# Down projection of a gated MLP from seven block products per pair of tiles, its token sums made during the up projection and its weight sums on the vector engine

## The chip, the cores and the metric

One core of a Trainium2 chip. The time is the device time of one execution in microseconds; the kernel before was run three times, and the median counts. One further execution was profiled. Everything is fp32.

## The reference, cut to what matters

The program is a block of a conformer/RWKV model followed by a two-layer block with attention and experts. The change touches the end of the first block only, its convolution-gated MLP over T = 16 + 512 = 528 tokens, with a width of 1024 and D_FF = 2816:

```python
def conv_gated_mlp(h, ffn_up, ffn_dw, ffn_down):
    u = causal_dwconv(h @ ffn_up, ffn_dw)
    return (jax.nn.silu(u[..., D_FF:]) * u[..., :D_FF]) @ ffn_down

h = layer_norm(ALPHA * h + conv_gated_mlp(h, ffn_up[l], ffn_dw[l], ffn_down[l]), ln2_g[l], ln2_b[l])
```

## The kernel before, in words

Activations lie with channels on the 128 partitions and tokens along the free dimension: `h` is 8 tiles of 128 x 528, the gated activation (`F_`) is 22 tiles (FT = 22). Tokens are cut into two halves of C1 = 264. Each engine has its own instruction queue, written out in order; semaphores tie them together. SP (SyncE) issues the weight transfers, PE (TensorE) multiplies, ACT (ScalarE) copies out of PSUM and computes silu, DVE (VectorE) does the rest and POOL (GpSimd) some weight sums.

**Weights** come in slabs into two slots of SBUF, in turn (`stream`, L330). A slab is requested when the slab before the last, which had the same slot, has been multiplied.

**The up projection** (`Seven`) treats 22 pairs of output tiles. A pair (the two halves of the gated unit for tile m) has a 2 x 2 block of weights (two halves of the contraction by two output tiles) and two token halves, so it is a 2 x 2 by 2 x 2 block product. It is made from seven products of half the contraction (4 weight tiles) each, in this order on PE (`seven_products`, products on L466): M1 into bank a, M2 into bank b, M6 added to a, M5 into c, M7 added to a, M3 added to c, and a last one added to a. Some products take sums of weight blocks, of token blocks or both. The weight sums are s1, s2, s3 (`seven_first_sums`, L427, L429, L430) and s4 (`seven_last_sum`, L437, in place, after M2); POOL makes them in the up projection. The token sums t1 to t4 (`token_sum`) DVE makes once ahead of the up projection. ACT copies the bank away after M1, M6 and M5 (`seven_copy`, L498), since the next product is added to it; DVE combines: c11 (L511) after M2, c22 (L518) after M7, c12 (L524) after M3; ACT takes c21 at the end (L2811). The last product of a pair waits for c22 to have read bank a.

Per pair DVE then runs six taps of the causal convolution for the pair before (`ffn_taps`, L3103 and L3106), ACT its silu (L2800), and DVE the gating multiplication one pair later (`ffn_gate`, L3091, counted by `ffn_f`). Halves (`up_u`) and tap results (`up_conv`) have four buffers each.

**Between the projections** PE makes 16 transposes of the context (L2608, into banks 4 to 7), and ACT copies six of its eight tiles away (L2816).

**The down projection** is `Dense`: 8 output tiles, one weight tile column of 22 x 128 x 128 (1408 KB) as a slab for each; per output tile PE runs 2 token halves x 22 products (L371) after it has waited for all 22 gated tiles. ACT copies each output tile (L2820) and DVE adds it to `ALPHA * h` (L3124, counted by `res2`). The layer norm behind it begins on PE (L553) when all eight are added.

Of the kernel before, what the change touches and what calls it, by code (L numbers as in the profile page):

```python
# [184 lines left out]
def build(nc, I, out):  # L185
# [69 lines left out]
    def pc(name, i=0, p1=P):  # L255
# [30 lines left out]
        "ffn_up": Seven(11, 4, KT, two, dmas=2), "ffn_down": Dense(8, 1, FT, two),  # L286
# [167 lines left out]
    def seven_products(pe, p, sums, x, t, cn, t0, first=None, between=None):  # L454
# [4 lines left out]
        block = seven_landed(pe, p)  # L459
        s1, s2 = sums(p)  # L460

        def product(bank, w, v, fresh, k0=None):
            for k in range(h):
                if k0 is not None and first:
                    pe.wait_ge(*first(k0 + k))
                mm = pe.matmul(PS[:, bank, 0:cn], w[:, k, :], v[:, k, :], start=fresh and k == 0, stop=k == h - 1,  # L466
                               skip_group_check=not fresh)
            return mm
# [8 lines left out]
        pe.wait_ge(S("sv_t"), t0 + 2)  # L477
# [5 lines left out]
        pe.wait_ge(S("sv_t"), t0 + 3)  # L483
# [5 lines left out]
        pe.wait_ge(S("sv_t"), t0 + 4)  # L489
# [43 lines left out]
    def halves(ap):  # L533
        return ap.rearrange("p (c n) -> p c n", c=2)
# [1637 lines left out]
    UP_T, UP_S = CS, BNS  # L2172
    UP_C = UP_S + 4 * KT // 2 * P
    assert UP_C + 3 * C1 <= TMP
# [16 lines left out]
    def _(sp):  # L2191
# [81 lines left out]
        def ffn_src(n, dst):  # L2273
# [8 lines left out]
        stream(sp, "ffn_down", lambda n, dst: [(  # L2282
            dst[:, 0:FT * P].rearrange("p (k n) -> p k n", k=FT),
            down[:, :, n * P:n * P + P] if isinstance(n, int) else down[:, :, ds(n * P, P)])])
# [11 lines left out]
    def _(pe):  # L2296
# [314 lines left out]
        products(pe, "ffn_down", lambda k, c0, cn: at(F_ + k * T1 + c0, cn), [(S("ffn_f"), FT)])  # L2611
# [3 lines left out]
    def _(act):  # L2615
# [187 lines left out]
        for m, p in enumerate(ffn7):  # L2803
# [5 lines left out]
            if m >= 4:  # L2809
                act.wait_ge(S("ffn_conv"), 2 * (m - 4) + 2)  # L2810
# [7 lines left out]
        for k in range(KT - 2):  # L2818
            ctx_take(k)
        take(act, "ffn_down", lambda i, acc, j: nc.scalar.activation(halves(at(i * T1 + UB, T1)), acc, ACT.Copy),  # L2820
             pre=[(S("ffn_f"), FT)])
# [39 lines left out]
    def _(dve):  # L2861
# [217 lines left out]
        V.memset(A[:, UB:UB + 8 * UW].rearrange("p (i t) -> p i t", t=UW)[:, :, 0:FFN_K - 1], 0.0).then_inc(S("ffn_zero"), 1)  # L3079
# [13 lines left out]
        def ffn_taps(m):  # L3093
            dve.wait_ge(S("sv_c"), 2 * ffn7[m].g + 2)
            dve.wait_ge(S("acc_free"), FREE0 + ffn7[m].tile + 2)
            if m >= 4:
                dve.wait_ge(S("ffn_f"), m - 3)
# [10 lines left out]

        for m in range(FT):
# [4 lines left out]
            if m >= 4:  # L3114
                dve.wait_ge(S("ffn_conv"), 2 * (m - 4) + 2)
# [6 lines left out]
        for i in range(KT):  # L3122
            dve.wait_ge(*taken("ffn_down", i + 1))
            V.scalar_tensor_tensor(out=at(hk(i), T1), in0=at(hk(i), T1), scalar=ALPHA, in1=at(UB + i * T1, T1),  # L3124
                                   op0=ALU.mult, op1=ALU.add).then_inc(S("res2"), 1)
# [37 lines left out]
```

## Time and profile before

| What | Value |
|---|---|
| median of 3 runs | 4442.01 us (4436.71 to 4442.95) |
| profiled execution, own time | 4433.85 us |
| its span | 4431.7 us |
| PE busy | 4145.6 us, 94% of the span |
| DVE busy | 1463.7 us, 33% |
| ACT busy | 1031.9 us, 23% |
| POOL busy | 558.0 us, 13% |
| up projection, about | 1084 to 1361 us |
| down projection, about | 1367 to 1526 us |

The span is from the first to the last profiled instruction; the execution's own time is 2.2 us longer. Engine shares are averages over all stages, so for a change in one stage its own stretch has to be read. In the profile one fp32 product of 128x128 by 128x264 appears as two MATMUL records. LDWEIGHTS (PEld) overlaps the products. "Idle before" names the time that an engine stood before an instruction and what released it.

### The profile page before, as it was taken

The numbers are of one execution on the slowest core, as the hardware profiler recorded it, in microseconds if no ns is written. First come the engines' busy times: TensorE is split into PE (matmuls) and PEld (weight loads), VectorE is DVE, ScalarE is ACT, GpSimd is POOL, SyncE is SP. The second block draws the span as 40 slices with busy tenths as digits, with TensorE's granted clock in tenths as the row PEclk, the third lists the DMA queues.
The fourth block names the chain that finished last, engine by engine and source line by source line (L and its number), as shares of the span: only waits on it lengthen the run. The fifth ranks groups of instructions, "written<-read, shape, count | busy, mean of one in ns | idle before, by whom it ended". The sixth has DMA issues, their size and how long they took to land. (4 is left out here: it accounts for less than half of the span.)

```text
span 4431.7 us, 64143 instructions
## 1 busy us (share of the span) xinstructions
PE 4145.6 (94%) x28308; PEld 2685.2 (61%) x28308; DVE 1463.7 (33%) x2272; ACT 1031.9 (23%) x2070; POOL 558.0 (13%) x476
## 2 busy tenths in 40 slices
PE   7999999999999989898999979999899989969888
PEld 5888789887888745555555533333355468843332
DVE  1385854352441112415633410000314064421112
ACT  2112522211110131514311221221314052121111
POOL 0000023101441000001223210100000024400000
PEclk9999999999999999999999989999999999989999
DMA  2584300212222212010011299999311101279997
GB/s 88 179 282 158 87 23 4 81 57 71 93 79 66 77 35 64 20 43 20 20 57 59 98 356 386 384 386 391 101 57 46 43 27 70 95 302 427 426 427 313
DMA packets 191429, 664.55 MB, mean 150 GB/s; under 512 B 11558, under 2 KB 75750, under 8 KB 166582
## 3 DMA queue, kind: packets, MB, share of 16 engines
q1 hardware_dynamic: 184950, 638.24, 38.0%
q0 software_dynamic: 6208, 22.27, 1.7%
q8 instruction: 222, 3.64, 0.3%
q14 instruction: 49, 0.40, 0.0%
HBM read 638.85 MB, written 20.05 MB: 149 GB/s over the span
## 5 line engine op out<-in xcount | busy, mean ns | idle before, releaser
L371 PE MATMUL psum<-arena 128*128 128x264 f32 (+4 forms) x3936 | 1026.6, 422 | 38.9 <-ACT arena L1301 19.1
L466 PE MATMUL psum<-arena 128*128 128x264 f32 (+2 forms) x3696 | 945.8, 418 | 12.5 <-ACT arena L2792 6.7
L371 PEld LDWEIGHTS psum<-arena 128*128 128x128 f32 x3936 | 747.2, 191 | 304.9 <-issue 123.1
L466 PEld LDWEIGHTS psum<-arena 128*128 128x128 f32 x3696 | 700.1, 190 | 255.1 <-issue 13.5
L1191 PE MATMUL psum<-arena 128*64 128x512 f32 x3072 | 700.2, 602 | 44.3 <-DMA arena<-in_w_e 37.5
L1191 PEld LDWEIGHTS psum<-arena 128*64 128x64 f32 x3072 | 212.3, 138 | 469.5 <-issue 429.4
L2060 DVE TENSOR_TENSOR arena<-arena,psum 128x512 f32<-128x512 f32 x32 | 22.0, 688 | 802.6 <-PE psum L1197 543.9
L869 PE MATMUL psum<-arena 128*128 128x512 f32 x544 | 235.7, 592 | 0.0
L2415 PE MATMUL psum<-arena 64*64 64x64 f32 x7424 | 225.9, 219 | 8.1 <-issue 4.5
L2415 PEld LDWEIGHTS psum<-arena 64*64 64x64 f32 x7424 | 224.0, 135 | 11.2 <-issue 8.4
L498 ACT ACTIVATE arena<-psum 128x384 f32<-128x384 f32 (+2 forms) x234 | 99.2, 424 | 494.8 <-PE psum L466 466.8
L1197 PE MATMUL psum<-arena 128*32 128x256 f32 x3072 | 185.7, 382 | 0.0
L869 PEld LDWEIGHTS psum<-arena 128*128 128x128 f32 x544 | 103.2, 190 | 128.5 <-issue 127.7
L437 POOL TENSOR_TENSOR arena<-arena 128x512 f32<-128x512 f32 (+1 forms) x78 | 105.6, 1354 | 571.2 <-PE psum L466 571.2
L1197 PEld LDWEIGHTS psum<-arena 128*32 128x32 f32 x3072 | 90.0, 109 | 127.4 <-issue 77.9
L2885 DVE SCALAR_TENSOR_TENSOR arena<-arena 128x528 f32<-128x528 f32 x240 | 164.8, 761 | 0.0
L2078 DVE SCALAR_TENSOR_TENSOR arena<-psum,arena 128x512 f32<-128x512 f32 (+1 forms) x96 | 66.9, 706 | 187.5 <-PE psum L1158 169.0
L427 POOL TENSOR_TENSOR arena<-arena 128x512 f32<-128x512 f32 (+1 forms) x78 | 95.2, 1221 | 251.8 <-DMA arena<-in_ffn_up 239.3
L518 DVE TENSOR_TENSOR arena<-arena,psum 128x384 f32<-128x384 f32 (+2 forms) x78 | 36.7, 471 | 245.4 <-PE psum L466 245.4
L2370 PE MATMUL psum<-arena 128*128 128x264 f32 x512 | 117.4, 387 | 0.0
L1575 ACT ACTIVATE arena<-psum,arena 64x512 f32<-64x512 f32 x64 | 43.7, 683 | 291.7 <-PE psum L1197 165.6
L2370 PEld LDWEIGHTS psum<-arena 128*128 128x128 f32 x512 | 96.1, 189 | 19.2 <-ACT arena L2701 2.5
(378 smaller groups left out, 3847.4 us busy)
## 6 DMA issues: line engine op xcount, KB each, us to landing
arena<-in_w_e SPq DMA_DIRECT2D x192, 2048.0 KB, 17.3
arena<-in_w_in SPq DMA_DIRECT2D x38, 2048.0 KB, 8.1
arena<-in_w_ada SPq DMA_DIRECT2D x24, 2048.0 KB, 8.9
arena<-in_ffn_up SPq DMA_DIRECT2D x22, 1024.0 KB, 7.5
arena<-in_w_branch SPq DMA_DIRECT2D x6, 2048.0 KB, 7.8
arena<-in_ffn_down SPq DMA_DIRECT2D x8, 1408.0 KB, 7.1
arena<-in_w_in SPq DMA_DIRECT2D x16, 512.0 KB, 4.5
arena<-in_w_out SPq DMA_DIRECT2D x4, 2048.0 KB, 8.7
```

The costliest lines, as they stand in the source:

```text
L371: mm = pe.matmul(PS[0:m, 2 * region + c, 0:cn], w[0:kp, k, j * P:j * P + m], rhs(k, c0, cn), start=(k == 0), stop=(k == s.kt - 1))
L427: tt(s1, block(1, 0), block(1, 1), ALU.add).then_inc(S("sv_sum"), 1)
L437: tt(a12, a12, sums(p)[1], ALU.subtract).then_inc(S("sv_sum"), 1)
L466: mm = pe.matmul(PS[:, bank, 0:cn], w[:, k, :], v[:, k, :], start=fresh and k == 0, stop=k == h - 1, skip_group_check=not fresh)
L498: nc.scalar.activation(dst, PS[:, c if made == M5 else a, 0:cn], ACT.Copy).then_inc(S("sv_cp"), 1)
L869: mm = pe.matmul(PS[:, 2 * r, :], at(tokens + t * P, P), w[:, k, :], start=(k == 0), stop=(k == KT - 1))
L1191: mm = pe.matmul(PS[c * HD:c * HD + HD, b + (m > 0), :], x(kk), w[:, k, c * BW:c * BW + BW], start=(kk == 0), stop=(kk == KT - 1))
L1197: mm = pe.matmul(PS[c * 32:c * 32 + 32, b + 2, (m > 0) * CTX:(m > 0) * CTX + CTX], xc(kk), w[:, k, c * CTX:c * CTX + CTX], start=(kk == 0) ...
L2078: inc(V.scalar_tensor_tensor(out=x, in0=PS[:, 6 + i % 2, 0:cn], scalar=mod(5, i, kind), in1=x, op0=ALU.mult, op1=ALU.add), "moe_res")
L2370: mm = pe.matmul(PS[:, 6 + c, 0:C1], at(gate_w[g % 3] + k * P, P), rhs_h(k, c * C1, C1), start=(k == 0), stop=(k == KT - 1))
L2415: mm = pe.matmul(PS[p0:p0 + HD, bank, i * CH:i * CH + CH], lhs(i, p0), rhs(i, p0), start=(j == 0), stop=(j == len(terms) - 1))
L2885: nc.vector.scalar_tensor_tensor(out=at(ck(k), T1), in0=at(j + ak(k), T1), scalar=pc("conv_w", n), in1=at(ck(k), T1), op0=ALU.mult, op1=AL ...
```

## The change

The down projection becomes `Seven` too: 4 pairs of output tiles, each from seven products of 11 weight tiles. Both output tiles' columns are needed at once: the first lies in the slot (`cols=P`), the second in one of two new areas (`DOWN_W`), loaded by a transfer of its own (`w_second0`, `w_second1`). The areas, and those for weight sums, token sums and outputs, are places in the arena that are free by then; the up projection's buffers for halves and taps go from four to two to make room.

- SP: the second tile of pair 0 is requested right behind the last up slab; the second tile of pair 1 only after the context's transposes and the last gated tile; pairs 2 and 3 request both tiles when the pair two before has ended.
- PE: pair 0 waits for gated tile k ahead of its product k, no longer for all of them; M6 waits for 32, M7 for 33, the last product for 44 of the token sums (`down_t`).
- DVE: `down_token_sums(m)` of gated tile m is run in the up projection three iterations after its pair: one operation of 128x264 for the first 11 tiles, two for the others; the last three tiles' sums follow behind the last gates, and then 11 operations for t4. The first three weight sums of pair 0 (128x1408 each) stand between the last up combination and the last taps. In each down pair DVE also makes s4, the combinations, the next pair's first three weight sums and two residual steps (one after c12, one after ACT's copy).
- ACT: three copies per pair and one copy of the last quarter (264 wide), in place of one copy of 528 per tile.

```diff
-        "ffn_up": Seven(11, 4, KT, two, dmas=2), "ffn_down": Dense(8, 1, FT, two),
+        "ffn_up": Seven(11, 4, KT, two, dmas=2), "ffn_down": Seven(4, 2, FT, two, cols=P),
...
-    def seven_landed(eng, p):
+    def seven_landed(eng, p, second=True):
         eng.wait_ge(S(f"w_in{p.q}"), p.landed)
+        if p.second and second:
+            eng.wait_ge(S(p.second[1]), p.second[2])
         w = slot[p.q][:, 0:p.kt * p.cols].rearrange("p (k n) -> p k n", k=p.kt)
         def block(i, j):
+            if i and p.second:
+                return at(p.second[0] + j * p.kt // 2 * P, p.kt // 2 * P).rearrange("p (k n) -> p k n", n=P)
             return w[:, j * p.kt // 2:(j + 1) * p.kt // 2, p.c + i * p.far:p.c + i * p.far + P]
...
-    up_u = lambda m, i: UB + (2 * (m % 4) + i) * UW
+    up_u = lambda m, i: UB + (2 * (m % 2) + i) * UW
-    up_conv = lambda m, i: FC + (2 * (m % 4) + i) * T1
+    up_conv = lambda m, i: FC + (2 * (m % 2) + i) * T1
+    down_ready = lambda i: (S("down_t"), (0, HALF, 3 * HALF - 1, 3 * HALF, 4 * HALF)[i])
...
+        for n, p in enumerate(down7):
+            if n == 0:
+                down_tile(at(p.second[0], FT * P), 1).then_inc(S(p.second[1]), 16)
+                sp.wait_ge(S("acc_full"), FULL0 + st["ffn_down"].last0[p.q])
+            elif n == 1:
+                sp.wait_ge(S("acc_full"), FULL0 + st["ffn_down"].last0[p.q])
+            else:
+                sp.wait_ge(S("acc_full"), FULL0 + down7[n - 2].tile + 2)
+            down_tile(slot[p.q], 2 * n).then_inc(S(f"w_in{p.q}"), 16)
+            if n == 1:
+                sp.wait_ge(S("ctx_turned"), KT)
+                sp.wait_ge(S("ffn_f"), FT)
+            if n:
+                down_tile(at(p.second[0], FT * P), 2 * n + 1).then_inc(S(p.second[1]), 16)
...
-        products(pe, "ffn_down", lambda k, c0, cn: at(F_ + k * T1 + c0, cn), [(S("ffn_f"), FT)])
+        for n, p in enumerate(down7):
+            seven_products(pe, p, down_sums, down_x, down_t, C1, down_ready,
+                           first=None if n else lambda k: (S("ffn_f"), k + 1))
...
-            if m >= 4:
-                dve.wait_ge(S("ffn_f"), m - 3)
+            if m >= 2:
+                dve.wait_ge(S("ffn_f"), m - 1)
...
+        def down_token_sums(m):
+            b1, b2 = (at(F_ + m * T1 + c * C1, C1) for c in range(2))
+            dve.wait_ge(S("ffn_f"), m + 1)
+            if m < HALF:
+                V.tensor_tensor(down_t(1)[:, m, :], b2, b1, ALU.subtract).then_inc(S("down_t"), 1)
+            else:
+                k = m - HALF
+                dve.wait_ge(S("down_t"), k + 1)
+                V.tensor_tensor(down_t(2)[:, k, :], b2, down_t(1)[:, k, :], ALU.subtract).then_inc(S("down_t"), 1)
+                V.tensor_tensor(down_t(3)[:, k, :], b2, down_t(3)[:, k, :], ALU.subtract).then_inc(S("down_t"), 1)
+
         for m in range(FT):
             if m:
                 ffn_taps(m - 1)
             if m >= 2:
                 ffn_gate(m - 2)
+            if m >= 3:
+                down_token_sums(m - 3)
...
+        seven_first_sums(dve, V.tensor_tensor, down7[0], down_sums)
         ffn_taps(FT - 1)
         ffn_gate(FT - 2)
+        down_token_sums(FT - 3)
         ffn_gate(FT - 1)
+        down_token_sums(FT - 2)
+        down_token_sums(FT - 1)
+        for k in range(HALF):
+            dve.wait_ge(S("down_t"), HALF + 2 * k + 1)
+            V.tensor_tensor(down_t(4)[k], down_x(1, 0)[:, k, :], down_t(2)[:, k, :], ALU.subtract).then_inc(S("down_t"), 1)
+        for n, p in enumerate(down7):
+            seven_last_sum(dve, V.tensor_tensor, p, down_sums)
+            seven_c11(dve, p, up_parts[0], C1, at(down_out(n, 0), C1))
+            if n + 1 < len(down7):
+                seven_first_sums(dve, V.tensor_tensor, down7[n + 1], down_sums)
+            seven_c22(dve, p, up_parts[2], C1, at(down_out(n, 1) + C1, C1))
+            seven_c12(dve, p, up_parts[1], C1, at(down_out(n, 0) + C1, C1))
+            for i in range(2):
+                if i == 0:
+                    dve.wait_ge(S("sv_c"), 2 * p.g + 2)
+                else:
+                    dve.wait_ge(S("acc_free"), FREE0 + p.tile + 2)
+                k = 2 * n + i
+                V.scalar_tensor_tensor(out=at(hk(k), T1), in0=at(hk(k), T1), scalar=ALPHA, in1=at(down_out(n, i), T1),
+                                       op0=ALU.mult, op1=ALU.add).then_inc(S("res2"), 1)
```

## Rows read from the trace of the kernel before

**Rows 1.** The page: busy us (share of the span) and instructions of each engine.

```profile
PE 4145.6 (94%) x28308; PEld 2685.2 (61%) x28308; DVE 1463.7 (33%) x2272; ACT 1031.9 (23%) x2070; POOL 558.0 (13%) x476
```

**Rows 2.** Timeline of the seam, 1320 to 1392: start us, us, engine, line, op, [idle before].

```profile
1352.61 2.15 POOL L437 TENSOR_TENSOR arena<-arena 128x512 f32<-128x512 f32 x1 [6.51 <-PE psum L466]
...
1359.60 0.43 DVE L524 TENSOR_TENSOR arena<-arena,psum 128x264 f32<-128x264 f32 x1 [1.35 <-PE psum L466]
...
1361.17 1.91 PE L2608 MATMUL psum<-arena 128*128 128x128 f32 x16
...
1361.86 0.90 DVE L3103 TENSOR_SCALAR arena<-arena 128x528 f32<-128x528 f32 x2 [1.83 <-ACT arena L2811]
...
1365.39 1.50 DVE L3091 TENSOR_TENSOR arena<-arena 128x528 f32<-128x528 f32 x2
1365.51 0.64 ACT L2800 ACTIVATE arena<-arena 128x528 f32<-128x528 f32 x1 [3.74 <-DVE arena L3106]
1366.05 1.74 ACT L2816 ACTIVATE arena<-psum 128x256 f32<-128x256 f32 x6
...
1366.94 25.32 PE L371 MATMUL psum<-arena 128*128 128x264 f32 x105 [3.86 <-DVE arena L3091]
```

**Rows 3.** Timeline of the end of the down projection, 1370 to 1620.

```profile
1525.68 0.61 ACT L2820 ACTIVATE arena<-psum 128x528 f32 x1 [18.97 <-PE psum L371]
1526.33 0.71 DVE L3124 SCALAR_TENSOR_TENSOR arena<-arena 128x528 f32<-128x528 f32 x1 [18.87 <-ACT arena L2820]
...
1527.09 7.39 PE L553 MATMUL psum<-arena 128*128 128x264 f32 x32 [1.55 <-DVE arena L3124]
```

**Rows 4.** Windows: us, busy of PE, PEld, DVE, ACT, POOL; clock, DMA share, GB/s.

```profile
1136.92:1149.39 12.47, 12.47 (x58) 10.62 (x57) 5.43 (x10) 2.10 (x5) 5.89 (x4) 1.00 0.51 168
...
1388.44:1408.02 19.58, 19.58 (x90) 16.72 (x89) 0.71 (x1) 0.61 (x1) 0.00 (x0) 1.00 0.28 74
1366.94:1388.44 21.50, 21.50 (x89) 18.05 (x90) 0.00 (x0) 0.85 (x4) 0.00 (x0) 0.92 0.03 7
1388.44:1525.54 137.10, 137.10 (x617) 116.73 (x615) 4.97 (x7) 4.28 (x7) 0.00 (x0) 1.00 0.28 79
```

**Rows 5.** Windows with PE alone behind the transposes: us, PE busy, clock, DMA.

```profile
1363.10:1366.90 3.80, 0.00 (x0) 1.00 1.14 301
...
1369.00:1371.00 2.00, 2.00 (x6) 0.50 0.00 0
```

**Rows 6.** Groups by shape, DVE, 1700 to 2300, and 1084 to 1560: busy, mean ns.

```profile
L448 DVE TENSOR_TENSOR arena<-arena 128x1536 f32<-128x1536 f32 x1 | 1.8, 1752 | 0.0
...
L451 DVE TENSOR_TENSOR arena<-arena 128x1056 f32<-128x1056 f32 x1 | 2.3, 2324 | 0.0
...
L448 DVE TENSOR_TENSOR arena<-arena 128x1056 f32<-128x1056 f32 x1 | 1.3, 1252 | 0.0
```

**Rows 7.** DMA issues of the page (KB each, us to landing) and SP's timeline.

```profile
arena<-in_w_in SPq DMA_DIRECT2D x38, 2048.0 KB, 8.1
...
arena<-in_ffn_down SPq DMA_DIRECT2D x8, 1408.0 KB, 7.1
...
1336.44 52.59 SPq L330 DMA_DIRECT2D arena<-in_ffn_down  x3
```

**Rows 8.** Timeline of one pair of the up projection, 1136 to 1150.

```profile
1140.75 2.16 POOL L437 TENSOR_TENSOR arena<-arena 128x512 f32<-128x512 f32 x1 [6.49 <-PE psum L466]
1141.08 0.70 DVE L3091 TENSOR_TENSOR arena<-arena 128x528 f32<-128x528 f32 x1
...
1142.39 0.39 ACT L498 ACTIVATE arena<-psum 128x264 f32<-128x264 f32 x1 [3.17 <-PE psum L466]
1142.87 1.27 POOL L427 TENSOR_TENSOR arena<-arena 128x512 f32<-128x512 f32 x1
...
1145.95 0.43 DVE L518 TENSOR_TENSOR arena<-arena,psum 128x264 f32<-128x264 f32 x1 [3.83 <-PE psum L466]
1147.73 0.43 DVE L524 TENSOR_TENSOR arena<-arena,psum 128x264 f32<-128x264 f32 x1 [1.35 <-PE psum L466]
```

More of the change, by code:

```diff
@@ L146, in __init__ @@
         self.kt, self.cols, self.c, self.far = kt, cols, c * P, far * P
+        self.second = None
 def plan(stages):
@@ L458, in seven_products @@
         free = FREE0 + p.tile
-        block = seven_landed(pe, p)
+        block = seven_landed(pe, p, second=False)
         s1, s2 = sums(p)
+        ready = t0 if callable(t0) else lambda i: (S("sv_t"), t0 + i)
         def product(bank, w, v, fresh, k0=None):
@@ L465, in product @@
                     pe.wait_ge(*first(k0 + k))
-                mm = pe.matmul(PS[:, bank, 0:cn], w[:, k, :], v[:, k, :], start=fresh and k == 0, stop=k == h - 1,
+                tile = v[k] if isinstance(v, list) else v[:, k, :]
+                mm = pe.matmul(PS[:, bank, 0:cn], w[:, k, :], tile, start=fresh and k == 0, stop=k == h - 1,
                                skip_group_check=not fresh)
@@ L476, in seven_products @@
         pe.wait_ge(S("sv_cp"), 3 * p.g + P_DONE)
-        pe.wait_ge(S("sv_t"), t0 + 2)
+        pe.wait_ge(*ready(2))
         product(a, s2, t(2), False).then_inc(S("sv_pe"), 1)
@@ L482, in seven_products @@
         pe.wait_ge(S("sv_cp"), 3 * p.g + Q_DONE)
-        pe.wait_ge(S("sv_t"), t0 + 3)
+        pe.wait_ge(*ready(3))
         product(a, block(1, 0), t(3), False).then_inc(S("sv_pe"), 1)
@@ L488, in seven_products @@
         pe.wait_ge(S("acc_free"), free + 1)
-        pe.wait_ge(S("sv_t"), t0 + 4)
+        pe.wait_ge(*ready(4))
         product(a, block(1, 1), t(4), False).then_inc(S("acc_full"), 2)
@@ L2171, in build @@
     UB, UW, FC, F_ = R_, T1 + FFN_K - 1, B_, K_
-    UP_T, UP_S = CS, BNS
-    UP_C = UP_S + 4 * KT // 2 * P
-    assert UP_C + 3 * C1 <= TMP
+    HALF = FT // 2
+    DOWN_W = [FC + 4 * T1, RAW]
+    DOWN_O = X2 + (KT - 3) * T2 + CTX + C1
+    DOWN_S = [(DOWN_O + 4 * T1, DOWN_W[0] + FT * P), (RAW + FT * P, DOWN_W[0] + FT * P + HALF * P)]
+    UP_C = DOWN_S[0][0] + HALF * P
+    UP_T, UP_S = CS, DOWN_S[1][1]
+    DOWN_T = UP_S + 4 * KT // 2 * P
+    DOWN_T4 = [X2 + k * T2 + CTX for k in range(KT - 2)] + [UP_S + HALF * P + k * C1 for k in range(2)]
+    DOWN_T4 += [DOWN_T + 2 * HALF * C1 + k * C1 for k in range(HALF - KT)]
+    assert UP_C + 3 * C1 <= F_ and F_ + FT * T1 <= RAW and RAW + (FT + HALF) * P <= DOWN_W[0]
+    assert UP_S + HALF * P + 2 * C1 <= DOWN_T and DOWN_T4[-1] + C1 <= 53200
     ffn7 = st["ffn_up"].pairs
@@ L2281, in _, with down_tile @@
         down = I["ffn_down"][0].rearrange("(k p) n -> p k n", p=P)
[L2282 to L2284 removed]
+        def down_tile(dst, i):
+            return sp.dma_start(dst[:, 0:FT * P].rearrange("p (k n) -> p k n", k=FT), down[:, :, i * P:i * P + P])
+        for n, p in enumerate(down7):
[12 more added lines that the diff above has]
+                down_tile(at(p.second[0], FT * P), 2 * n + 1).then_inc(S(p.second[1]), 16)
         first_slabs(sp, 0)
@@ L2819, in _ @@
             ctx_take(k)
-        take(act, "ffn_down", lambda i, acc, j: nc.scalar.activation(halves(at(i * T1 + UB, T1)), acc, ACT.Copy),
-             pre=[(S("ffn_f"), FT)])
+        for n, p in enumerate(down7):
+            for made, part in zip((M1, M6, M5), up_parts):
+                seven_copy(act, p, made, part, C1)
+            a = seven_last(act, p)
+            if n >= 2:
+                act.wait_ge(S("res2"), 2 * (n - 2) + 2)
+            nc.scalar.activation(at(down_out(n, 1), C1), PS[:, a, 0:C1], ACT.Copy).then_inc(S("acc_free"), 1)
         act.wait_ge(S("res2"), KT)
```

22 lines of the change are left out of this document (13 added, 9 removed).

## The prediction

> **What bounds the kernel now.** I read the page first: TensorE (PE) is busy for 94% of the span [rows 1], so a change of the multiplication count can pay, if the stretch concerned is bound by PE too. Then I read the timeline from the end of the up projection to the layer norm behind the down projection. Its rows show the seam: the 16 transposes of the context end at 1363.08 us, PE stands idle for 3.86 us until VectorE (DVE) has made the last gated tile, and then runs the down projection without a gap from 1366.94 [rows 2] to 1525.54, where the last copy, the last residual step and the next norm follow [rows 3]. The windows show what the stretch is made of: seven of the eight output tiles take 137.10 us, one takes 19.58, all at full clock, while DVE is busy for 5 us and ACT for 4 [rows 4]. A tile is 2 chunks x 22 products, so one 128x128 by 128x264 product costs 19.58 / 44 = 0.445 us. The first tile takes 21.50 at a mean clock of 0.92 [rows 4]: behind the idle stretch the granted clock is 0.50, which is the 1.2 GHz level, and later 1.00, the 2.4 GHz one [rows 5]. So down projection and seam are bound by PE, but for 3.86 us of waiting for DVE and about 1.9 us of half clock that the wait causes.
>
> **The change, part by part.**
>
> *Block products.* A pair of output tiles needs 4 block products of 11 weight tiles times 2 (44 x 2 = 88 products); it will need 7 x 11 = 77. Four pairs: 308 instead of 352. Does a product keep its price in the seven-product form? The up projection has that form already: 7 x 4 = 28 products in 12.47 us, 0.445 us each, with all the waits between products in it [rows 4]. So the 308 cost 308 x 0.4453 = 137.1 us, which is also what the last 308 products take now [rows 4]. Before, the 352 take 1525.54 - 1366.94 = 158.6 us. Gain 21.5 us, of which 19.6 are the 44 products and 1.9 the half-clock start, if PE comes without the idle stretch.
>
> *The seam on PE.* The first pair waits for gated tile k alone before its product k, 22 waits instead of one for all. So it may begin when the transposes end, at 1363.1 instead of 1366.94, 3.8 us earlier. M1 (11 products) ends at 1368.0, M2 at 1372.9. The waits themselves I take at nothing, as the 15 or so in each up pair cost nothing visible; if each of the 22 cost 0.06 us, it would be 1.3 us.
>
> *The seam on DVE.* This is where a new wait could appear, so I follow the queue. The last c12 starts at 1359.60 and ends at 1360.03 [rows 2]. Behind it now stand three weight sums of 128x1408. The rows give 1.25 us for 1056 columns and 1.75 for 1536, so 1.62 by the straight line between them [rows 6]; three make 4.85 and end at 1364.9. Both weight tiles are there: the slot's tile is issued at 1336.44 as now and lands after 7.1 us [rows 7], the other is issued behind the last up slab, at about 1361.2 - 4 x 12.47 = 1311.3. The six taps, now 1361.86 to 1365.39 [rows 2], take 3.53 us and end at 1368.4, 3.0 us later than now. Gate 20 (0.7) and the two sums of tile 19 end at 1369.8. A token sum of 264 columns is 0.43 us by the combining operations of that width, about 0.36 start to start [rows 8]. ACT's last silu (0.64) is over at 1369.1 and hides behind them. Gate 21 ends at 1370.4, where M2 wants tile 21 at 1372.4: 2 us to spare. The third product M6 needs the last sum t2, at about 1371.5, where PE arrives at 1372.9: 1.4 us to spare. ACT comes to copy M1 after silu and six context copies (1.74 us [rows 2]), at 1370.9, ready at 1371.3: 1.6 us to spare. So the three added sums cost nothing, hidden under M1 and M2, which are 9.8 us of PE work; if that cover were gone they would cost their 4.85 us plus the sums of the tail.
>
> *Then t4 and the rest.* Eleven more token sums (4 us) end near 1376.3, the last weight sum (it waits for M2) at 1378, c11 at 1378.4. PE wants S4 at the sixth product, 1387.6. For pair 1 SP holds its second tile back until all 22 gated tiles exist, 1370.4; landed at 1377.5; queued behind that wait are pair 2's tiles, which wait for the end of pair 0 (1397.4) anyway. In the steady pairs DVE has per pair 4 weight sums x 1.62, three combinations x 0.43 and two residual steps x 0.71: 9.2 us in 34.3. Pairs 2 and 3 get two tiles of 1408 KB each, issued when the pair two before ends. One after the other they take 2 x 7.1 = 14.2 us, by the step from 1408 KB (7.1) to 2048 KB (8.1) together only 9.3 [rows 7]. Add 4.85 us of sums: 19.1 us at worst, and the first thing that PE would miss is the release of the accumulator by c22, due when M7 ends, 5 x 4.9 = 24.5 us into the pair. Hidden with 5 us to spare.
>
> *Up projection.* Per pair DVE gets one token sum (tiles 0 to 10) or two (11 to 18), in 19 pairs. They stand between gate and c11. DVE is idle there for 3.83 us before c22 [rows 8]; 0.4 to 0.8 us go into that hole, and c11 moves later, which nobody awaits before the pair's end. The buffers for halves and taps shrink from four to two; each reuse waits for work that DVE or ACT did one iteration before (gate m-2 stands ahead of taps m on the same queue), so nothing. POOL's last sum, 2.16 us beside the gate's operation against 1.27 for its others, may stretch again by the length of the sums; it ends at 1142.9 and PE wants it at the sixth product, 5 x 1.78 us after 1136.9 = 1145.8. The tile issued behind the last up slab at 1311.3 shares that slab's transfer time; POOL wants the slab at 1142.87 + 15 x 12.47 = 1329.9, 18 us later.
>
> The Trainium skill, SBUF — State Buffer, section "Who interferes with whom", says that a DVE instruction with two SBUF inputs and a GpSimd instruction that reads SBUF exclude each other, and the later one fully blocks. Here the gate, started 0.33 us after the POOL operation, keeps its 0.70 us and POOL's is the longer one [rows 8], so the trace bears out a contention but not that the later one waits. By the page's rule the sums would each stand behind a POOL operation; that is the third rival.
>
> *The end.* The last copy is 264 columns (0.39 us [rows 8]) instead of 528 (0.61), the rest is the same: 0.2 us gained [rows 3]. Nothing behind waits for more: both slabs of the next layer are issued earlier.
>
> *Sum.* 21.5 + 3.8 + 0.2 = 25.5 us. The down projection ends at 1500.2, and the norm's first product starts at 1501.5 instead of 1527.09. The profiled execution took 4433.85 us (span 4431.7), so it would be 4408.3; the median of the runs is 8.2 us higher, 4442.0, and I predict 4442.0 - 25.5 = 4416.5.
>
> **The rivals.**
>
> *PE waits at the seam.* Beside POOL's work an added sum can cost 2.32 instead of 1.25 us [rows 6], a factor 1.85. POOL's last operation starts at 1352.61 [rows 2], so nothing speaks for it here, but the margins are only 1.4 to 2 us. With the factor on the three sums (4.1 us more) and the tail's token sums (2 more), t2 would be ready at 1377.5, PE would stand for 4.6 us in all and run at half clock again for 1.9 us of loss. Gain 19, time 4423.
>
> *Weights come late in the pairs.* The point at which it costs is a landing later than 24.5 - 4.85 = 19.6 us after issue. At double the serial time (28.4) c22 would be 8.8 us late in up to three pairs, 26 us: all the gain, 4442. Against it: the transfers of this stretch land in 7.1 us each with the engines three quarters idle [rows 4].
>
> *Token sums stand behind POOL's in the up projection.* If both sums waited for all four POOL operations (until 1146.7), c11 and c22 would end at 1148.2, 0.5 us past PE's need at 1147.7; over 8 pairs with two sums, and 0.1 us over 11 with one, 5 us. Time 4421.5.
>
> *DVE becomes the bound of the up projection* (the one that ends slower). DVE is busy 5.43 of 12.47 us per pair [rows 4] and has 3.83 + 1.35 us before c22 is late. A loss of 25.5 us over 19 pairs is 1.34 us each, so from sums of 3.83 + 1.35 + 1.34 = 6.5 us per pair the change is no gain (4442), and at 7.1 us it is 11 us slower (4453). That is ten to twenty times the 0.4 to 0.8 us that they cost by the rows, and no row shows such a factor.
>
> **How the numbers follow.** Measurement tells about 0.2%, 9 us, from nothing. The forecast gets 0.71, PE waiting at the seam 0.16, sums behind POOL 0.06, late weights 0.04 (of which 0.03 end within 0.2%), DVE as bound 0.03 (0.01 within, 0.02 slower). That is 0.94 faster, 0.04 same, 0.02 slower. The range goes from 4411 (the lowest run of before less 25.5; no step can yield more) to 4425 (the seam's rival and its bounds, the 1.3 us of waits, and 1 us of scatter).
>
> **What would show it.** Right: 616 PE records in the down projection instead of 704, 34.3 us per pair; PE follows the transposes with no gap and no clock below 1.00; the up pair stays at 12.47 us; DVE idle before c22 shrinks to 3.0 to 3.5 us; the next norm's first product starts 140.3 us after the first transpose (1361.2), instead of 165.9. Wrong: an idle PE in front of M6 or of the last product of a pair, released by DVE; a clock of 0.5 behind 1361; up pairs over 12.5 us.

## The result and the profile after

| | changed | before | ratio, 95% interval |
|---|---|---|---|
| median of 4 runs each | 4412.1 us (4410.06 to 4412.77) | 4442.48 us | 0.9933 (0.9916 to 0.995) |
| profiled execution | 4412.77 us, span 4410.9 | 4433.85 us, span 4431.7 | |

The kernel became 30.4 us faster in the medians (0.7%), and 21 us in the two profiled executions. Both differ from the 25.5 of the prediction, so the stage has to be read by itself. The kernel before had medians of 4436.7 to 4440.0 us in the four later sets of runs, so its first median, 4442.48, lay high, and some of the 30.4 us is scatter. The page after, whose PE row answers to [rows 1]: 21 us less PE time.

```profile
span 4410.9 us, 64037 instructions
...
PE 4124.3 (94%) x28220; PEld 2665.5 (60%) x28220; DVE 1510.5 (34%) x2344; ACT 1032.0 (23%) x2078; POOL 566.4 (13%) x476
```

The timeline of the changed kernel, 1340 to 1540, from the seam to the next norm (as [rows 2] and [rows 3]; L473 is now the product of both projections, L525 c22, L432 to L435 and L442 the weight sums, L3164 and L3165 token sums, L3188 t4, L2648 the transposes):

```profile
1358.23 1.62 DVE L432 TENSOR_TENSOR arena<-arena 128x1408 f32<-128x1408 f32 x1
...
1359.46 1.91 PE L2648 MATMUL psum<-arena 128*128 128x128 f32 x16
...
1361.21 137.22 PE L473 MATMUL psum<-arena 128*128 128x264 f32 x616
1361.42 1.62 DVE L435 TENSOR_TENSOR arena<-arena 128x1408 f32<-128x1408 f32 x1
1362.96 0.90 DVE L3150 TENSOR_SCALAR arena<-arena 128x528 f32<-128x528 f32 x2
...
1367.79 0.70 DVE L3138 TENSOR_TENSOR arena<-arena 128x528 f32<-128x528 f32 x1
...
1368.73 0.44 ACT L505 ACTIVATE arena<-psum 128x264 f32<-128x264 f32 x1
...
1369.10 0.43 DVE L3164 TENSOR_TENSOR arena<-arena 128x264 f32<-128x264 f32 x1
...
1369.78 3.87 DVE L3188 TENSOR_TENSOR arena<-arena 128x264 f32<-128x264 f32 x11
...
1407.81 1.63 DVE L432 TENSOR_TENSOR arena<-arena 128x1408 f32<-128x1408 f32 x1 [0.28 <-DMA arena<-in_ffn_down]
...
1498.89 0.71 DVE L3202 SCALAR_TENSOR_TENSOR arena<-arena 128x528 f32<-128x528 f32 x1 [4.14 <-ACT arena L2868]
...
1499.66 7.39 PE L560 MATMUL psum<-arena 128*128 128x264 f32 x32 [1.22 <-DVE arena L3202]
```

PE runs 616 records in 137.22 us with no idle stretch and follows the transposes at once. DVE's last gate (1367.79) and its last t2 (1369.10, over at 1369.5) are done before PE arrives at M6, two times 4.9 us after 1361.2, at 1371.0. The windows of the changed kernel (as [rows 4]) show the clock at 1.00 where it was 0.50 [rows 5], and a middle pair of 34.3 us in which DVE is busy for 9.0:

```profile
1366.00:1370.00 4.00, 4.00 (x20) 3.42 (x19) 4.00 (x10) 2.57 (x8) 0.00 (x0) 1.00 0.06 15
...
1397.40:1431.70 34.30, 34.30 (x156) 29.30 (x155) 9.02 (x9) 1.56 (x4) 0.00 (x0) 1.00 0.34 84
```

**A yardstick for all runs.** From the first transpose of the context to the norm's first product it was 1527.09 - 1361.17 = 165.92 us [rows 2, 3], and is 1499.66 - 1359.46 = 140.20: 25.72 us less. This length returned to 0.01 us in a second profile of the same kernel. What follows, by unchanged code, took from 2904.6 us (before) to 2912.0 us (late2) in the twelve profiles whose code is the same there, 2911.2 in the changed kernel's. That scatter is as large as most effects below, so they are read from the stage, and the medians only say whether they agree. It also explains the 20.8 us between the two profiled spans: 1.7 us were gained ahead of the first transpose, 25.7 in the stage, and 6.6 were lost again behind it, in code that is the same.

The up projection kept its pace: 19 pairs took 1359.66 - 1122.87 = 236.79 us by ACT's last copies, 12.46 each, and 1361.38 - 1124.59 = 236.79 before. One of its pairs in the timeline of the changed kernel, to be held against [rows 8]:

```profile
1350.90 2.84 POOL L442 TENSOR_TENSOR arena<-arena 128x512 f32<-128x512 f32 x1 [5.82 <-PE psum L473]
1351.22 0.70 DVE L3138 TENSOR_TENSOR arena<-arena 128x528 f32<-128x528 f32 x1
1351.84 0.43 DVE L3164 TENSOR_TENSOR arena<-arena 128x264 f32<-128x264 f32 x1
1352.18 0.43 DVE L3165 TENSOR_TENSOR arena<-arena 128x264 f32<-128x264 f32 x1
...
1356.10 0.43 DVE L525 TENSOR_TENSOR arena<-arena,psum 128x264 f32<-128x264 f32 x1 [3.16 <-PE psum L473]
```

The two sums took 0.67 us out of DVE's hole before c22 (3.83 to 3.16), and POOL's last sum grew from 2.16 to 2.84 us, by just their time. In both kernels it ended 1.13 us after the end of the last DVE operation with two inputs in SBUF, the gate before (1141.78 and 1142.91) and the second sum now (1352.61 and 1353.74).

### The profile page after: what moved, and what is told of

The parts are those of the page before. It is cut to its first block and busy times, and to the rows that moved or that the text cites. A ratio compares the mean times of both kernels' runs of the same rounds, so it can differ in the third digit from the quotient of the medians.

```text
span 4410.9 us, 64037 instructions
## 1 busy us (share of the span) xinstructions
PE 4124.3 (94%) x28220; PEld 2665.5 (60%) x28220; DVE 1510.5 (34%) x2344; ACT 1032.0 (23%) x2078; POOL 566.4 (13%) x476
## 5 line engine op out<-in xcount | busy, mean ns | idle before, releaser
L473 PE MATMUL psum<-arena 128*128 128x264 f32 (+2 forms) x4312 | 1083.6, 414 | 12.0 <-ACT arena L2834 6.7
L473 PEld LDWEIGHTS psum<-arena 128*128 128x128 f32 x4312 | 817.7, 190 | 274.6 <-issue 12.7
L372 PE MATMUL psum<-arena 128*128 128x264 f32 (+4 forms) x3232 | 869.1, 429 | 35.2 <-ACT arena L1308 19.1
L372 PEld LDWEIGHTS psum<-arena 128*128 128x128 f32 x3232 | 612.9, 191 | 278.2 <-issue 120.3
L442 POOL TENSOR_TENSOR arena<-arena 128x512 f32<-128x512 f32 (+1 forms) x78 | 114.4, 1466 | 564.1 <-PE psum L473 564.1
L876 PEld LDWEIGHTS psum<-arena 128*128 128x128 f32 x544 | 103.2, 190 | 128.5 <-issue 127.7
L525 DVE TENSOR_TENSOR arena<-arena,psum 128x384 f32<-128x384 f32 (+2 forms) x82 | 38.5, 469 | 267.0 <-PE psum L473 267.0
L432 POOL TENSOR_TENSOR arena<-arena 128x512 f32<-128x512 f32 (+1 forms) x78 | 95.0, 1218 | 249.6 <-DMA arena<-in_ffn_up 237.6
L2410 PEld LDWEIGHTS psum<-arena 128*128 128x128 f32 x512 | 96.1, 189 | 19.2 <-ACT arena L2743 2.5
```

Of the source, the lines that this page charges most:

```text
L372: mm = pe.matmul(PS[0:m, 2 * region + c, 0:cn], w[0:kp, k, j * P:j * P + m], rhs(k, c0, cn), start=(k == 0), stop=(k == s.kt - 1))
L432: tt(s1, block(1, 0), block(1, 1), ALU.add).then_inc(S("sv_sum"), 1)
L442: tt(a12, a12, sums(p)[1], ALU.subtract).then_inc(S("sv_sum"), 1)
L473: mm = pe.matmul(PS[:, bank, 0:cn], w[:, k, :], tile, start=fresh and k == 0, stop=k == h - 1, skip_group_check=not fresh)
L876: mm = pe.matmul(PS[:, 2 * r, :], at(tokens + t * P, P), w[:, k, :], start=(k == 0), stop=(k == KT - 1))
L2410: mm = pe.matmul(PS[:, 6 + c, 0:C1], at(gate_w[g % 3] + k * P, P), rhs_h(k, c * C1, C1), start=(k == 0), stop=(k == KT - 1))
```

## Experiments

Medians in us, the kernel before beside each, on the same chip; "stage" is the yardstick, "19 pairs" the time of the up pairs that carry token sums, 236.8 us before and in the changed kernel.

| run | median | before | ratio, 95% | stage | 19 pairs |
|---|---|---|---|---|---|
| after_again | 4412.96 | 4439.96 | 0.9938 (0.9924 to 0.9952) | 140.19 | 236.8 |
| dense_early | 4430.74 | 4439.96 | 0.9986 (0.9977 to 0.9995) | 160.11 | |
| seven_late | 4416.26 | 4439.96 | 0.9954 (0.994 to 0.9967) | 149.08 | |
| pool_sums | 4409.76 | 4439.96 | 0.9932 (0.9918 to 0.9946) | 140.20 | |
| sums_last | 4412.23 | 4439.9 | 0.994 (0.9923 to 0.9956) | 140.20 | |
| late2 | 4417.47 | 4439.9 | 0.9948 (0.9931 to 0.9964) | 148.23 | |
| extra3 | 4456.9 | 4439.9 | 1.0038 (1.0024 to 1.0052) | 140.20 | 279.1 |
| extra6 | 4545.74 | 4439.9 | 1.0235 (1.0218 to 1.0252) | 141.36 | 367.0 |
| psum3 | 4413.85 | 4436.73 | 0.9948 (0.9933 to 0.9964) | 140.19 | 240.3 |
| psum6 | 4442.46 | 4436.73 | 1.0011 (1.0002 to 1.002) | 140.20 | 265.6 |
| turn_late | 4412.4 | 4436.73 | 0.9945 (0.9931 to 0.9958) | | |
| turn_late2 | 4414.58 | 4438.14 | 0.9943 (0.993 to 0.9957) | | |

### Is the stage all of the gain: after_again

The changed kernel without an edit.

> The changed kernel once more, as the reference of the others. In the stage the two profiles differ by 25.5 us (the norm's first product 27.4 us earlier, 1.9 of them already there ahead of the up projection), the medians by 30.4. If the stage is all of it, the difference of the medians is 25 to 26 us within the scatter of 4 us; if something outside the stage gained too, it stays near 30.

The medians differ by 27.0 us, the stage is 140.19. So nothing outside the stage gained that could be shown; 25.7 lies inside both intervals (22 to 37 us and 21 to 34).

### What the early start is worth alone: dense_early

```diff
-        products(pe, "ffn_down", lambda k, c0, cn: at(F_ + k * T1 + c0, cn), [(S("ffn_f"), FT)])
+        products(pe, "ffn_down", lambda k, c0, cn: at(F_ + k * T1 + c0, cn), first=lambda k: (S("ffn_f"), k + 1))
```

(in the kernel before)

> The kernel before with one edit: the first output tile of its down projection waits for gated tile k ahead of product k instead of for all 22. Theory: 3.8 us of idle time and 1.9 us of half clock are bought by this wait alone, so 5.7 us less than before, about 4437, no clock under 1.00 behind the transposes, 352 products in 156.7 us; the other 19.8 us belong to the seven products. Rival: the per-tile waits only work together with the new form, because the last gated tile ends at 1366.9 and PE would stall inside the first tile: gain under 2 us.

```profile
1358.73 1.91 PE L2608 MATMUL psum<-arena 128*128 128x128 f32 x16
...
1360.48 21.75 PE L371 MATMUL psum<-arena 128*128 128x264 f32 x97
```

That timeline shows the products close up behind the transposes. The stage is 160.11, 5.81 less than before; expected were 5.7. The medians say 9.2 us with an interval of 2 to 10. So 5.8 of the 25.7 us need no block products at all: one wait was split. The other 19.9 are the 44 products saved (19.6) and the shorter last copy.

### The seven products without the early start: seven_late

```diff
-                           first=None if n else lambda k: (S("ffn_f"), k + 1))
+                           first=None if n else lambda k: (S("ffn_f"), FT))
```

> The changed kernel with one edit: pair 0 waits for all 22 gated tiles before its first product. DVE's last gate now ends at 1368.5, since the weight sums stand ahead of the taps, and PE is ready at 1361.2. Theory: 7.3 us idle and again 1.9 us of half clock, 9.2 us more than the changed kernel, about 4421, and the gain of seven products left is 21 us. Rival: the half clock does not return or costs nothing, because the up projection and transposes ran up to it: 7.3 us. Second rival: the stall takes work off later waits: under 4 us.

Timeline, then windows (PE alone: us, busy, clock, DMA), of seven_late:

```profile
1368.51 13.86 PE L473 MATMUL psum<-arena 128*128 128x264 f32 x55 [7.27 <-DVE arena L3138]
```

```profile
1368.50:1370.50 2.00, 1.99 (x5) 0.50 0.36 107
...
1372.50:1374.50 2.00, 2.00 (x11) 1.00 1.10 277
```

The stage grew by 8.88 us. PE's first product came 7.4 us later behind the transposes, nearly all of it idle (7.27), and the 616 records took 138.69 us instead of 137.22, so half clock cost 1.5. Both terms of the seam are shown, the second smaller than the 1.9 expected. The gain left is 16.8 us by the stage (165.92 - 149.08), not 21: that figure had been counted from the difference of the medians. The medians differ by only 3.3 us; the runs of this kernel spread over 11 us.

### Which engine makes the weight sums, and in which order: pool_sums and sums_last

pool_sums moves all weight sums of the down projection to POOL:

```diff
+            for p in down7:
+                seven_first_sums(pool, nc.gpsimd.tensor_tensor, p, down_sums)
+                seven_last_sum(pool, nc.gpsimd.tensor_tensor, p, down_sums)
...
-        seven_first_sums(dve, V.tensor_tensor, down7[0], down_sums)
...
-            seven_last_sum(dve, V.tensor_tensor, p, down_sums)
```

> The changed kernel with all weight sums of the down projection on POOL (which is idle there) in place of DVE. Theory: they are hidden on either engine. POOL takes 1.27 us for 512 columns, so about 3.4 us for 1408, 13.7 us per pair of 34.3; pair 0's are made from 1354 on, and S2 is wanted at 1371. Same time as the changed kernel within 0.1%, DVE's last gate about 4.9 us earlier. Rival: POOL's sums come late for M6 of pair 0, since DVE's taps and gates hold them up: PE idles before M6, 2 to 6 us more.

The stage is 140.20, so the place of the sums is free. But DVE's last gate was not earlier: it came 8.4 us after the first transpose, 8.3 in the changed kernel. The timeline shows why:

```profile
1363.60 3.17 POOL L435 TENSOR_TENSOR arena<-arena 128x1408 f32<-128x1408 f32 x1
1363.67 3.81 DVE L3153 TENSOR_SCALAR arena<-arena 128x528 f32<-128x528 f32 x2 [1.83 <-ACT arena L2853]
```

DVE was rid of 4.85 us of sums. 1.8 of them went into waiting for ACT's copy of the last quarter, which the taps need (1.83 us idle; in the changed kernel the sums cover it). The other 2.9 went behind POOL: the two first taps (0.90 us in the changed kernel) started 0.07 us after POOL's third sum and took 3.81. So moving the sums away gave DVE nothing.

sums_last puts the three sums of pair 0 behind the last token sums:

```diff
-        seven_first_sums(dve, V.tensor_tensor, down7[0], down_sums)
         ffn_taps(FT - 1)
...
         down_token_sums(FT - 1)
+        seven_first_sums(dve, V.tensor_tensor, down7[0], down_sums)
```

> The changed kernel with the three weight sums of pair 0 behind the last token sums in place of ahead of the last taps. Theory: both orders are hidden under M1 and M2. DVE's last gate is 4.9 us earlier less a wait for ACT, s2 is there at about 1370.4 where PE wants it at 1371.0: same time as the changed kernel. Rival: s2 is the last thing now and late, PE idles 0.5 to 2 us before M6.

```profile
1364.39 1.62 DVE L432 TENSOR_TENSOR arena<-arena 128x1408 f32<-128x1408 f32 x1
1366.04 1.62 DVE L434 TENSOR_TENSOR arena<-arena 128x1408 f32<-128x1408 f32 x1
```

In its timeline s2 is over at 1367.7, 0.7 us before M6 (1368.4, two products of 4.9 us after 1358.6). Stage 140.20: no cost either way, with a little more than half a microsecond to spare.

### How late the weights may be: late2

```diff
                 sp.wait_ge(S("acc_full"), FULL0 + down7[n - 2].tile + 2)
+                for e in range(2):
+                    down_tile(slot[p.q], 2 * n).then_inc(S("w_extra"), 16)
+                    sp.wait_ge(S("w_extra"), 16 * (2 * (n - 2) + e + 1))
```

> The changed kernel with two superfluous transfers of 1408 KB, one after the other and each awaited by SP, ahead of the two tiles of down pairs 2 and 3: about 14.2 us later. In the changed kernel both tiles land 12.2 us after issue. The prediction's deadline was c22 at the end of M7, 24.5 us into the pair: 12.2 + 14.2 + 4.85 - 24.5 = 6.8 us late, two pairs 13.5 us, and half clock behind each stall, 1.9 each, 17 us. Rival: c22 is awaited by the last product only, 29.4 us into the pair, so c22 has to be over by then: 31.3 + 0.4 - 29.4 = 2.2 us late, two pairs 4.5 us, without a fall of the clock.

Timeline and windows (PE alone) of late2:

```profile
1422.93 1.63 DVE L432 TENSOR_TENSOR arena<-arena 128x1408 f32<-128x1408 f32 x1 [14.29 <-DMA arena<-in_ffn_down]
...
1428.14 36.22 PE L473 MATMUL psum<-arena 128*128 128x264 f32 x154 [2.02 <-DVE arena L525]
```

```profile
1426.10:1428.10 2.00, 0.02 (x1) 1.00 0.00 0
...
1430.00:1432.00 2.00, 2.00 (x6) 0.50 0.00 0
```

Neither theory was right as a whole. PE stood for 2.0 us in each of the two pairs, 4.1 in all, which is the rival's deadline (the last product, 29.4 us into the pair) and not the prediction's. But the clock did fall behind each stall: the stage is 8.0 us longer, and 3.9 of them are not idle time but longer products. Some 0.5 of that is how a stall reads at full clock too (psum6 below: 0.27 us for each), so half clock cost about 3.4, nearly as much as the standing.

### How much DVE work the up pairs can take: extra3, extra6, psum3, psum6

extra3 and extra6 add three or six DVE operations with an unused result ahead of the token sums of tiles 0 to 18:

```diff
             dve.wait_ge(S("ffn_f"), m + 1)
+            for e in range(3 if m < FT - 3 else 0):
+                dve.wait_ge(S("extra"), 3 * m + e)
+                V.tensor_tensor(at(DOWN_T + 2 * HALF * C1, 3 * C1), at(H, 3 * C1), at(H + 3 * C1, 3 * C1), ALU.subtract)\
+                    .then_inc(S("extra"), 1)
```

psum3 and psum6 differ from them in one operand:

```diff
-                V.tensor_tensor(at(DOWN_T + 2 * HALF * C1, 3 * C1), at(H, 3 * C1), at(H + 3 * C1, 3 * C1), ALU.subtract)\
+                V.tensor_tensor(halves(at(DOWN_T + 2 * HALF * C1, 3 * C1)), halves(at(H, 3 * C1)), PS[:, 4:6, 0:396], ALU.subtract)\
```

> The changed kernel with three more DVE additions of 128x792 (both inputs in SBUF, result unused) per pair in front of the token sums of tiles 0 to 18: 3 x 1.04 = 3.1 us of DVE time in 19 of the 22 up pairs. The prediction let them fall into DVE's hole before c22 (3.5 us with one sum, 3.16 with two, and 1.35 more until PE misses c22): no cost, up pairs of 12.47 us. Theory of the port: POOL's last sum L442 stands still while DVE reads two inputs from SBUF. It grew from 2.16 to 2.50 and 2.84 us with one and two sums, 0.34 each, the sums' own time. Then it grows to 5.6 and 5.9 us, ends 0.6 to 0.9 us after the 8.9 us at which PE wants s4, and 19 pairs cost 11 x 0.6 + 8 x 0.9 = 14 us. By the rule that the later one waits (SBUF - State Buffer of the Trainium skill) DVE's additions would get longer, not POOL's.

> As extra3 with six additions, 6.2 us per pair, the price that the prediction named as the point where the change gains nothing (6.5 us). By DVE's hole alone c22 ends 1.5 to 1.9 us late, 19 pairs cost 32 us: stage as slow as the kernel before. Theory of the port: L442 takes 8.7 to 9.1 us and s4 is 3.7 to 4.0 us late, so 19 pairs cost 73 us, 4485.

Both theories failed: 19 pairs took 42.3 us more in extra3, 130.2 in extra6. A pair near the end of the up projection in the timeline of extra3:

```profile
1340.13 4.91 DVE L3161 TENSOR_TENSOR arena<-arena 128x792 f32<-128x792 f32 x3
...
1344.27 1.89 POOL L434 TENSOR_TENSOR arena<-arena 128x512 f32<-128x512 f32 x1
1344.96 1.50 DVE L3168 TENSOR_TENSOR arena<-arena 128x264 f32<-128x264 f32 x1
1346.13 1.45 POOL L435 TENSOR_TENSOR arena<-arena 128x512 f32<-128x512 f32 x1
1346.38 1.48 DVE L3169 TENSOR_TENSOR arena<-arena 128x264 f32<-128x264 f32 x1
...
1348.60 14.41 PE L473 MATMUL psum<-arena 128*128 128x264 f32 x56 [2.15 <-DVE arena L525]
```

PE waits for c22, not for POOL's s4, and DVE is late since its own operations have grown: three additions take 4.91 us, and the token sums 1.5 us each in place of 0.43. Each token sum started 0.25 to 0.7 us after a POOL operation and ended 0.3 after its end (1346.16 and 1346.46; 1347.58 and 1347.86). DVE had waited until POOL was through. Of the three additions the first, without a gap behind the gate, took 0.97 us, and the second and third 1.93 and 1.94: by the edit each waits for the one before, and starts some 0.04 us after its end. A new theory followed, that only operations with two inputs from SBUF wait:

> extra3 with one of the two inputs of each addition taken from PSUM (two idle banks) in place of SBUF; width, count and place are the same, so DVE's own time is the same, 3 x 1.04 us a pair. In extra3 19 pairs cost 44 us in all: the additions took 4.9 us instead of 3.1 and the token sums behind them 1.5 us each instead of 0.43, each ending as a POOL operation ended. Theory of the port: only operations with two SBUF inputs wait for POOL. Then these take 3.1 us, fall into DVE's hole before c22 (3.16 us and 1.35 more), and pairs stay at 12.47 us: the time of the changed kernel, about 4412. Rival: any 3 us of DVE work in this place cost this much, by the queue: about 4456.

> extra6 with one input from PSUM. Theory of the port and the hole: 6.2 us against 3.5 (11 pairs) or 3.16 (8 pairs) and 1.35 more, c22 late by 1.4 to 1.7 us, 11 x 1.4 + 8 x 1.7 = 29 us more than the changed kernel, about 4441, and up to 2 us per pair more where the clock falls behind a stall. The two token sums behind them may stand beside POOL's operations: 1 us each. Rival: as extra6, 133 us more.

Timelines of psum3 and of psum6:

```profile
1332.64 2.99 DVE L3161 TENSOR_TENSOR arena<-arena,psum 128x792 f32<-128x792 f32 x3
...
1333.81 1.27 POOL L432 TENSOR_TENSOR arena<-arena 128x512 f32<-128x512 f32 x1
...
1335.55 1.17 DVE L3168 TENSOR_TENSOR arena<-arena 128x264 f32<-128x264 f32 x1
...
1338.87 11.39 PE L473 MATMUL psum<-arena 128*128 128x264 f32 x50 [0.23 <-DVE arena L525]
```

```profile
1323.59 6.04 DVE L3161 TENSOR_TENSOR arena<-arena,psum 128x792 f32<-128x792 f32 x6
...
1329.55 0.43 DVE L3168 TENSOR_TENSOR arena<-arena 128x264 f32<-128x264 f32 x1
...
1331.05 12.73 PE L473 MATMUL psum<-arena 128*128 128x264 f32 x56 [1.45 <-DVE arena L525]
```

The same number of additions now takes 2.99 us, and POOL's sums 1.27 as if alone. psum3 costs 3.5 us in 19 pairs: 12.46 each with one sum, 12.96 in seven of the eight with two (12.47 in the last), since the two token sums still meet POOL's operations (1.17 and 1.49 us). psum6 costs 28.8 us, 13.83 and 14.18 a pair, 1.4 and 1.7 more than 12.46 as expected. Its token sums come after POOL's work and take 0.43 again. So the hole before c22 was sized rightly, and what the prediction lacked is that two-input operations can queue behind POOL's.

The clock has a part in the two large costs. PE alone over the 19 pairs (us, busy, clock, DMA) of the changed kernel, extra3, extra6 and psum6:

```profile
1122.87:1359.66 236.79, 236.79 (x1066) 1.00 0.27 84
...
1133.63:1412.70 279.07, 251.72 (x1066) 0.96 0.23 71
...
1126.20:1493.23 367.03, 280.34 (x1066) 0.85 0.18 54
...
1124.26:1389.84 265.58, 241.88 (x1066) 1.00 0.24 75
```

The same 1066 records are busy for 5.1 us more in psum6, where the clock never fell: 0.27 us for each of its 19 stalls. In extra3 they are busy for 14.9 us more and in extra6 for 43.6. Less the same 5.1, half clock cost about 10 of the 42.3 us and about 38 of the 130.2; the rest is DVE's lateness. Without the clock's part extra3 would still lose 32 us and extra6 92, more than the 25.7 that the change gained.

### A seam without transposes: turn_late and turn_late2

Since PE bounds the stage, PE work that can be done in an idle stretch of PE is worth its time. turn_late loads the context after the last pair and turns it behind the norm's statistics (shown in part):

```diff
+        ln_pe(pe, hk, T1, [(S("res2"), KT)])
         pe.wait_ge(S("ctx_in"), 16)
+        pe.wait_ge(S("ln_var"), ln_n["pe"])
         for k in range(KT):
             for t in range(2):
...
...
-        ln_pe(pe, hk, T1, [(S("res2"), KT), (S("ctx_taken"), KT - 2)])
...
+        def ln2_put(k):
+            if k == 0:
+                for i in range(KT):
+                    ctx_take(i)
```

> The changed kernel with the 16 transposes of the context (and ACT's eight copies of them) moved out of the seam into the norm behind the down projection, where PE stands idle for 16 us after the statistics; the context is loaded into the same place after the last pair. Theory: the seam is bound by PE alone now, so 1.9 us of PE work go: 1.9 us less between the last up pair and the norm's first product, and the next layer's norm 1.9 us earlier too, since the copies fit between ACT's root and its first scaled tile. Rival: ACT's copies (2.3 us) or the late load hold up the scaled tiles, and the 1.9 us are lost again before the next layer. In the medians neither can be seen.

```profile
1372.74 127.51 PE L473 MATMUL psum<-arena 128*128 128x264 f32 x572 [0.26 <-DVE arena L3165]
...
1524.00 2.32 ACT L2859 ACTIVATE arena<-psum 128x256 f32<-128x256 f32 x8 [4.26 <-DVE arena L591]
```

From ACT's last up copy (1362.73) to the norm (1501.47) it was 138.74 us, 1.26 less than the changed kernel's 140.00; PE now waits 0.26 us for the last t2, and DVE's tail has become the bound of the seam. To the next layer's first square sum (1536.26) it was 173.53, 1.1 more than 172.44: the copies stood behind the wait for the first normed tile, and held up the scaled ones. The rival was right. turn_late2 mends both (its edit against turn_late, in part):

```diff
         nc.scalar.activation(at(LNB[1], t), at(LNB[1], t), ACT.Sqrt).then_inc(S("ln_sd"), 1)
+        if between:
+            between()
...
-        seven_first_sums(dve, V.tensor_tensor, down7[0], down_sums)
+        seven_first_sums(dve, V.tensor_tensor, down7[0], down_sums, part=0)
...
         down_token_sums(FT - 1)
+        seven_first_sums(dve, V.tensor_tensor, down7[0], down_sums, part=1)
```

(part 0 is s1 and s2, part 1 is s3; `between` is ACT's eight copies of the context)

> turn_late with two edits. ACT's eight context copies stand between its root and the wait for the first normed tile (there they stood behind that wait and cost 2.1 us); and of pair 0's three weight sums the third, wanted only by M7, follows the last token sums (there PE waited 0.26 us for a token sum and 0.4 more at the start, because DVE's tail had lost the cover of the transposes). Theory: nothing is late any more, so from the last up copy to the norm's first product 138.1 us (changed kernel 140.0, turn_late 138.7), and to the next layer's first square sum 170.5 (172.4 and 173.5). Rival: the copies still hold up the scaled tiles, 172 or more.

```profile
1364.43 0.39 ACT L2859 ACTIVATE arena<-psum 128x264 f32<-128x264 f32 x1 [4.42 <-PE psum L476]
...
1521.06 2.32 ACT L2864 ACTIVATE arena<-psum 128x256 f32<-128x256 f32 x8
...
1535.31 5.49 PE L570 MATMUL psum<-arena 128*128 128x384 f32 x8 [12.98 <-ACT arena L607]
```

The norm begins at 1502.67, 138.24 us after the last up copy, and the next layer's first square sum after 170.88: 1.8 and 1.6 us less than in the changed kernel. This is the shortest stage of all, but 1.6 us are 0.04% and the medians can't tell it from the changed kernel (4414.58 against 4412.1 and 4412.96, from other sets of runs).

## Why the prediction was right

**The sum.** Forecast 25.5 us for the stage, measured 25.72. The 308 products: 137.1 predicted, 137.22 measured. The early start with full clock: 3.8 + 1.9 = 5.7, measured alone 5.81. The end: 0.2 predicted; PE's idle before the norm went from 1.55 to 1.22 us, 0.3. The norm's first product was put 140.3 us after the first transpose and came after 140.20. The time of 4416.5 was 4.4 us above the median of 4412.1, and after_again and the scatter of the unchanged rest show no further gain that it missed. For the profiled execution 4408.3 was forecast, and it took 4412.77, with the code behind the stage 6.6 us slower than in the profile before. So the stage was forecast to 0.2 us by its mechanism; that the whole kernel's time came within 5 us is as good as its scatter allows.

**The seam's margins.** Each of the three ready times held within 0.4 us, counted from PE's start of M1 (1363.1 predicted, 1361.2 in the trace): gate 21 over at 7.3 (predicted 7.3), t2 at 8.3 (8.4), ACT's copy of M1 over at 8.0 (8.2). sums_last and pool_sums moved the added sums without cost; seven_late, which takes the cover away by making PE wait for DVE's tail, showed the price: 8.9 us. turn_late brings PE 1.75 us earlier and makes it wait 0.26 us for t2, so the slack of that order is about 1.5 us, as the 1.4 said.

**Late weights.** The step on the deadline was wrong: c22 need not be over when M7 ends but when the last product begins, 4.9 us later. Both tiles landed after 12.2 us (L432 at 1407.81 waits for them; the pair began at 1395.6), between the 9.3 and the 14.2 of the prediction, and the sums ended at 17, so there are 12 us to spare, not 5. The rival lost its small chance for a better reason than was given. It also priced lateness without the clock; in late2 the clock was over 40% of the cost.

**The port** (what makes DVE and POOL wait for each other). The prediction read from POOL's 2.16 us beside a gate of 0.70 [rows 8] that the later operation doesn't wait. The Trainium skill, SBUF — State Buffer, section "Who interferes with whom", says that two-input DVE operations and reading GpSimd operations exclude each other, the later one waiting to the end. extra3 and psum3 agree with it: 1.5 us for 0.43 with two SBUF inputs, 2.99 for 4.91 when one came from PSUM. The trace of the kernel before had shown it too. The 2.32 us of [rows 6] were taken for a factor of 1.85; in its place in the timeline the operation stands behind POOL's:

```profile
1090.24 2.40 POOL L437 TENSOR_TENSOR arena<-arena 128x512 f32<-128x512 f32 x1 [14.66 <-PE psum L466]
1090.26 1.25 DVE L448 TENSOR_TENSOR arena<-arena 128x1056 f32<-128x1056 f32 x1
...
1091.42 2.32 DVE L451 TENSOR_TENSOR arena<-arena 128x1056 f32<-128x1056 f32 x1
```

POOL's sum ended 1.13 us after L448, and L451 (a sum of 1.25 us) 1.10 us after POOL's: first POOL waited for DVE, then DVE for POOL. What hid this in the up pairs is that there POOL's operation was the one held up, by 0.34 us for each added sum, although its record starts 0.33 us before the gate's. The third rival, named after that rule, cost nothing in the changed kernel for this reason. Which of the two is held is not settled: gate and sums follow each other without a gap, and POOL waited for the last of them, but L451 followed L448 without a gap as well, and POOL came between. That the third rival cost nothing was therefore luck as far as the prediction goes: it had priced it at 5 us with a chance of 0.06, and had no row that said who would wait.

**The rival that ends slower** named 6.5 us of added DVE work per pair as the point of no gain. psum6, with about 6 us of work in addition to the sums, lies there (4442.46 against 4436.73). For operations with two SBUF inputs that each wait for the one before, the point is at most 3.1 us (three at 1.04) on top of the sums: extra3 is slower than before by 0.38%. The mechanism and the sign were right, but for such operations the threshold was at most about half as far away. Whether token sums in a row without a gap, as the change has them, would reach it as soon was not run; its one and two sums per pair cost nothing.

## What to carry to other kernels

Where a stage is bound by PE at full clock, count its products and price them by a row of the same form elsewhere in the kernel: seven block products for eight are worth 1/8 of the stage if every sum finds cover, and the form already in use next door shows the price of its waits. Before crediting such a change, look at what it also unties: here a wait split by tile gave 5.8 of 25.7 us and needed none of the algebra. Room on a half-idle DVE is not one number: beside a busy POOL an operation with two SBUF inputs can cost two to three times its row (1.93 us for 0.97, 1.5 for 0.43), with one input from PSUM it costs its row. And a late engine costs PE more than the wait, where the clock falls behind it: about 38 of 130 us in extra6.

## What the hardware showed unexpectedly

- A DVE `tensor_scalar` from SBUF to SBUF waits for POOL too: two of them took 3.81 us instead of 0.90 when they started 0.07 us after a POOL sum of 3.17 us (pool_sums). The first took 3.40 of it and ended 0.3 us after POOL's, as the token sums of extra3 did. It was seen in this one place.
- A stall of 2.0 us in a run of products was followed by a granted clock of 0.50 (the 1.2 GHz level) and cost nearly as much again as the stall itself (late2: 4.1 us idle, about 3.4 us by the clock). In seven_late 7.27 us of standing were followed by only 1.5 us of such loss, and in psum6 stalls of up to 1.45 us in 19 pairs by none: its clock stayed at 1.00.
- The same unchanged code behind the stage took 2904.6 to 2912.0 us in different executions, so a median of five runs can't show what a stage's own length shows to 0.01 us.
